# A two-layer hybrid encoder on one core: the weighted sum of the dilated branch's three patterns formed by Pool instead of DVE

## The chip, the cores and the metric

The kernel runs on one core of a Trainium2 chip. Its engines are TensorE (PE, matrix products and transposes), VectorE (DVE), ScalarE (ACT), GpSimd (Pool) and SyncE (SP), which here issues most DMAs. Each runs its own list of instructions in order and waits on semaphores. The metric is the device time of one execution in microseconds (us).

## The reference, cut to what matters

Two layers. In each, one input projection feeds four token mixers (A, B, C, D) and four gates. The outputs, projected and gated, are summed, projected and added to x; a gated MLP with a short convolution follows. The change concerns mixer C, which runs the same banded attention with three dilation patterns and weights their outputs per head with a softmax over the three log-sum-exps:

```
def dilated_attention(c_qkv, pos, q_norm, k_norm):
    ...
    for j, (window, r) in enumerate(C_PATTERNS):       # 3 patterns
        ...
        o, lse = banded_attention(strided(q)[:, :, :, None], strided(k), strided(v), strided(pos), ...)
        outs.append(unstrided(o[:, :, :, 0]))
        lses.append(unstrided(lse[:, :, :, 0]))
    w = jax.nn.softmax(jnp.stack(lses, 0), axis=0)
    o = jnp.sum(w[..., None] * jnp.stack(outs, 0).astype(jnp.float32), axis=0)
    return o.reshape(b, s, C_HEADS * HEAD_DIM).astype(c_qkv.dtype)
```

Sequence length is 512, C has 8 heads of 64 columns, all data is float32. So `o` is 512 x 512: four tiles of 128 tokens with 512 columns each, and three such sets go into the sum.

## The kernel before

**Dense work.** `ORDER` (line 130) lists the projections of a layer in the order in which PE does them. Each weight block is cut into tiles of 256 rows; SP loads them into two buffers `raw`. To keep float32 precision each weight tile is split in two: ACT makes the high half `wh` (line 833), DVE the low half `wl = raw - wh` (line 1262), and the same is done with activations (`hTh`/`hTl`, `gTh`/`gTl`). A product is then three matmuls (line 500). A tile of a block is four "slots" of PE, one for each PSUM bank, six matmuls each.

**The order of everything else.** Small work is woven between the slots. Each stream of an engine yields a due time counted in slots, and `together` takes the stream that is due first. This happens when the program is built, so on the chip each engine has one fixed list. The block before the change is `cq` (D's latent queries), then come `gate2a` (16 slots) and `dq0`. Behind `END["cq"]` these things are due:

- DVE: nine steps of an inverse square root by Newton (lines 1293 to 1299), four pairs of instructions that scale cq (lines 1470 and 1472, the second raises `normed`), the low halves of the turned cq tiles (line 1620), splits of weight tiles (1262), and the combination of C (`c_combine`): weights from the statistics (1395 to 1413), then for each of the four tiles three products with a weight broadcast over 64 columns (1419) and two sums (1422). The last sum of each tile raises `combined`.
- PE: a turn is a set of 128x128 transposes (line 530) into the single PSUM bank `TD`. It waits until ACT and DVE have taken the last one out (`td_act`, `td_dve`). Four turns of cq stand 6, 8, 10 and 12 slots behind `END["cq"]`, four of the combined C tiles at 14, 15.5, 17 and 18.5; the latter wait for `combined`.
- ACT: high halves of turned tiles (1032 for cq, 993 for C), and the eviction of `gate2a` (881) at 13.3 slots, which waits for `combined` of the fourth tile since its target `merged` lies over `oC`:

```
yield from gates_out("gate2a", merged[:, 0:4, :], combined.at(l, 4))
```

- Pool fills two buffers before the layers begin and has nothing to do in them.

Of the kernel before, what the change touches and what calls it, by code (L numbers as in the profile page):

```python
# [16 lines left out]
ALU = mybir.AluOpType  # L17
# [4 lines left out]
P = 128  # L22
# [3 lines left out]
HD = 64  # L26
# [80 lines left out]
class Own:  # L107
# [12 lines left out]
    pj_dve=108, sq_used=60, normed=53, combined=4, sublayer_normed=4, h_normed=8, td_ready=69, td_act=69, td_dve=69, nt_ready=16, nt_act=16,  # L120
    nt_dve=16, ta_ready=136, ta_act=136, ta_dve=136, q_padded=64, s_ready=144, s_biased=144, p_ready=144, b_mixed=16, o_ready=128, o_out=24,
    gains_in=1, ssum=16, lam_dot=1, lam_exp=1, c_diff=1, c_exp=1, merged_sum=24, merged_hi=8, merged_lo=8, conv_mid=44,
    e_ready=22, hidden_val=22, hidden_hi=22, hidden_lo=22, act_step=189, dve_step=497, params_in=16, direct_in=8,
    x_moved=2, c0_moved=6,
)

# [30 lines left out]
def build(nc, io):  # L157
    ctx = ExitStack()
    with ctx:
        _build(nc, io, ctx)  # L160
# [42 lines left out]
def _build(nc, io, ctx):  # L203
    def sb(name, shape, dt=F32):
        return ctx.enter_context(nc.sbuf_tensor("s_" + name, shape, dt))
# [3 lines left out]
    def signal(name, before=0, unit=1):  # L209
        s = Signal(ctx.enter_context(nc.semaphore(name)), before, EACH.get(name, 0), unit)  # L210
        signals[name] = s
        return s
# [25 lines left out]
    stat = sb("stat", [P, 16, 32])  # L238
# [5 lines left out]
    def in_work(at, n, **dims):  # L244

        names = " ".join(dims)
        return work[:, at:at + n].rearrange(f"p ({names} n) -> p {names} n", **dims)
# [7 lines left out]
    oC = in_work(AD + 6144, 6144, j=3, t=4)  # L255
# [42 lines left out]
    combined = signal("combined")  # L298
# [21 lines left out]
    lam_exp = signal("lam_exp")  # L320
    c_diff = signal("c_diff")
    c_exp = signal("c_exp")
    merged_sum = signal("merged_sum")
    merged_hi = signal("merged_hi")
    merged_lo = signal("merged_lo")
    conv_mid = signal("conv_mid")
    e_ready = signal("e_ready")
    hidden_val = signal("hidden_val")
    hidden_hi = signal("hidden_hi")
    hidden_lo = signal("hidden_lo")  # L330
    act_step = signal("act_step", before=1)
    dve_step = signal("dve_step", before=1)
    params_in = signal("params_in", before=16, unit=16)
    direct_in = signal("direct_in", unit=16)
# [15 lines left out]
    def layers(eng):  # L350
        return eng.Fori(0, DEPTH)
# [78 lines left out]
    @block_.sync  # L430
    def _(sp):
        for dst, src in ((work[:, 512:1024].bitcast(I32), io["positions"][0, :].partition_broadcast(P)),
                         (work[:, 256:260].bitcast(I32), io["positions"].rearrange("a (t p) -> p (a t)", p=P)),
                         (work[:, 260:264].bitcast(I32), io["positions"].rearrange("a (p r) -> p (a r)", r=RES)),
                         (consts[:], io["k_consts"])):
            sp.dma_start(dst, src, allow_slow_non_contiguous=True).then_inc(small_in, 16)
        sp.dma_start(x_sb, io["x"].rearrange("a (t p) n -> p (a t) n", p=P)).then_inc(x_in, 16)
        sp.wait_ge(rows_clear, 1)
        for dst, src in list(parameter_rows(0))[6:]:
            sp.dma_start(dst, src, allow_slow_non_contiguous=True).then_inc(params_in.handle, params_in.unit)  # L440
        for dst, src in ((near[:], io["k_near"]), (work[:, 0:256].rearrange("p (m n) -> p m n", m=2), io["k_mask_c12"])):
            sp.dma_start(dst, src).then_inc(setup_in, 16)
        with layers(sp) as l:
            for k, (_when, (pieces, chunks, cols, _last)) in enumerate(weight_tiles(l)):

                sp.wait_ge(*tile_split.at(l, k - 1))
                dst = raw[:, k % 2, 0:chunks * cols].rearrange("p (c n) -> p c n", c=chunks)
                for at, n, src in pieces:
                    sp.dma_start(dst[:, :, at:at + n], src).then_inc(*(raw_landed[k % 2]).up())

        sp.wait_ge(*pj_dve.at(DEPTH, 0))
        sp.dma_start(io["y"].rearrange("a (t p) n -> p (a t) n", p=P), x_sb).then_inc(out_done, 16)
        sp.wait_ge(out_done, 16)


    @block_.gpsimd
    def _(pool):

        for s in (tile_split, tile_used, pj_ready, pj_dve, td_act, td_dve, ta_act, ta_dve, s_biased, o_out, act_step, dve_step):
            pool.sem_inc(s.handle, s.before)  # L460
        pool.memset(rows[:], 1.0).then_inc(rows_clear, 1)
        pool.memset(q_pad[:], 0.0).then_inc(pad_clear, 1)


    @block_.tensor
# [736 lines left out]
    def _(dve):  # L1202
        v = nc.vector
# [47 lines left out]
        with layers(dve) as l:  # L1251
            n_ready, n_turn, n_unit, n_att, n_hi, n_act, n_norm = [0], [0], [0], [0], [0], [0], [0]
            own = Own(pj_dve)
# [57 lines left out]
            def heads(ap, h, w=None):  # L1311
                return ap.rearrange("p (h n) -> p h n", h=h)

            def over(col, n):

                return col.unsqueeze(2).to_broadcast([P, col.shape[1], n])
# [72 lines left out]
            def c_combine():  # L1389

                begin = END["cq"] + 0.3
                yield begin
                dve.wait_ge(*c0_moved.at(l, 6))
                dve.wait_ge(*own.done(l))
                v.tensor_tensor(stat[:, 15, :], stat[:, 5, :], stat[:, 6, :], ALU.min).then_inc(*dve_step.up(own))
                dve.wait_ge(*own.done(l))
                v.tensor_tensor(stat[:, 15, :], stat[:, 15, :], stat[:, 7, :], ALU.min).then_inc(*dve_step.up(own))
                for j in range(3):
                    dve.wait_ge(*own.done(l))
                    v.tensor_tensor(stat[:, 12 + j, :], stat[:, 15, :], stat[:, 5 + j, :], ALU.subtract).then_inc(*(c_diff if j == 2 else dve_step).up(own))  # L1400
                yield begin + 1.2
                dve.wait_ge(*c_exp.at(l, 1))
                dve.wait_ge(*own.done(l))
                v.tensor_tensor(stat[:, 8:11, :], stat[:, 8:11, :], stat[:, 12:15, :], ALU.mult).then_inc(*dve_step.up(own))
                dve.wait_ge(*own.done(l))
                v.tensor_tensor(stat[:, 8, :], stat[:, 8, :], stat[:, 9, :], ALU.add).then_inc(*dve_step.up(own))
                dve.wait_ge(*own.done(l))
                v.tensor_tensor(stat[:, 8, :], stat[:, 8, :], stat[:, 10, :], ALU.add).then_inc(*dve_step.up(own))
                dve.wait_ge(*own.done(l))
                v.reciprocal(stat[:, 8, :], stat[:, 8, :]).then_inc(*dve_step.up(own))  # L1410
                for j in range(3):
                    dve.wait_ge(*own.done(l))
                    v.tensor_tensor(stat[:, 12 + j, :], stat[:, 12 + j, :], stat[:, 8, :], ALU.mult).then_inc(*dve_step.up(own))
                for t in range(4):
                    for j in range(3):
                        yield begin + 5 + 2 * t + 0.6 * j
                        o = oC[:, j, t, :]
                        dve.wait_ge(*own.done(l))
                        v.tensor_tensor(heads(o, 8), heads(o, 8), over(stat[:, 12 + j, 8 * t:8 * t + 8], HD), ALU.mult).then_inc(*dve_step.up(own))  # L1419
                        if j:  # L1420
                            dve.wait_ge(*own.done(l))
                            v.tensor_tensor(oC[:, 0, t, :], oC[:, 0, t, :], o, ALU.add).then_inc(*(combined if j == 2 else dve_step).up(own))

            def add_to_x(names):
                for cb, name in enumerate(names):
# [303 lines left out]
            def attentions():  # L1729
# [44 lines left out]
                for j in (1, 2):  # L1774
                    yield from attention(f"C{j}", biased_residues(j), keep_residues(j), 2)
                yield from c_combine()
                yield from attention("D", biased_d, tile_of_heads(False), 8, tile_at=0)
                yield from attention("A", biased_near(0, A_SLOPES, floor=lambda u: sink[:, u % 8:u % 8 + 1]), tile_of_heads(True), 8,
# [47 lines left out]
```

## Time and profile before

| | |
|---|---|
| time, median of 3 runs | 2898.15 us (2895.33 to 2903.14) |
| profiled execution | span 2911.1 us; the profile gives no other time of it |
| mean granted TensorE clock | 0.960 |
| PE busy | 2729.1 us, 94% |
| DVE busy | 1567.2 us, 54% |
| ACT busy | 1221.1 us, 42% |
| Pool busy | 1.5 us |

A busy share is an average over the whole span. Rows in order of time begin with the start in us from the span's start and the duration in us; "x3" is three merged instructions, and a bracket holds the engine's idle time before the row and who ended it. The granted clock stands in tenths of full speed or as a share (1.00 is 2.4 GHz, 0.50 is 1.2 GHz).

### The profile page before, as it was taken

The page shows a single profiled execution, that of the slowest core. Times are in us where ns is not written, and L with a number is a line of the kernel's source. Part 1 is how long each engine was busy: PE and PEld are TensorE (multiplying, and loading weights), DVE is VectorE, ACT ScalarE, POOL GpSimd, SP SyncE. Part 2 cuts the span into 40 slices and gives each one's busy share as a digit, 9 for nine tenths or more (in the row PEclk, how much of TensorE's full clock was granted, in tenths as well). Part 3 has the DMA queues.
Part 4 walks back from the last instruction along what each step waited for, and adds up shares of the span by engine and source line. Part 5 has one row for each costly group of instructions (what it writes and reads, how often), then busy time and mean ns, then how long its engine had stood idle before and what let it go on. Part 6 is the DMA issues. An engine that isn't in the chain of part 4 may idle for free.

```text
span 2911.1 us, 44313 instructions
## 1 busy us (share of the span) xinstructions
PE 2729.1 (94%) x12974; PEld 2274.5 (78%) x12974; DVE 1567.2 (54%) x3226; ACT 1221.1 (42%) x2487; POOL 1.5 (0%) x6
## 2 busy tenths in 40 slices
PE   5999989889999998999989999898899999899998
PEld 4899877667777787888868998775677777788887
DVE  5454476435546546564655554754355545564745
ACT  4455544335543234342435455433355342342422
POOL 0000000000000000000000000000000000000000
PEclk9999999879999999999999999998699999999999
DMA  4212212001112332333332122220012223223332
GB/s 157 81 51 82 75 56 92 8 8 52 59 60 72 103 100 77 99 94 101 96 103 73 56 77 76 68 80 1 22 45 66 62 72 110 79 95 102 95 95 94
DMA packets 141881, 217.58 MB, mean 75 GB/s; under 512 B 14841, under 2 KB 69451, under 8 KB 141259
## 3 DMA queue, kind: packets, MB, share of 16 engines
q1 hardware_dynamic: 132585, 200.62, 22.2%
q10 hardware_dynamic: 9058, 14.06, 1.5%
q8 instruction: 116, 1.90, 0.3%
q14 instruction: 122, 1.00, 0.1%
HBM read 206.20 MB, written 8.45 MB: 74 GB/s over the span
## 4 chain that ended last, share of the span: by engine, by line
PE 78%; DVE 9%; issue 5%; ACT 5%; ACTq 1%; DMA 1%; DVEq 0%; SPq 0%
PE bank L500 60%; PE bank L693 5%; PE bank L530 5%; PE bank L683 5%; PE bank L737 2%; ACT s_wh L833 1%; DVE s_wl L1262 1%; PE bank L728 1%; DVE s_gTl L1589 1%; ACT s_work L1082 1%; DMA s_raw<-in_w_in 1%; DVE s_work L1419 1%; ACT s_gTh L993 1%; PE bank L566 1%; ACTq L933 1%
## 5 line engine op out<-in xcount | busy, mean ns | idle before, releaser
L1262 DVE TENSOR_TENSOR s_wl<-s_raw,s_wh 128x1024 fp32r<-128x1024 f32 (+2 forms) x376 | 454.4, 1209 | 518.3 <-ACT s_wh L833 515.2
L833 ACT ACTIVATE s_wh<-s_raw 128x1024 fp32r<-128x1024 f32 (+2 forms) x376 | 392.9, 1045 | 587.2 <-PE bank L500 569.2
L500 PE MATMUL bank<-s_hTh,s_wh 128*128 128x512 f32 x1216 | 502.7, 413 | 9.7 <-DVE s_work L1356 9.7
L500 PE MATMUL bank<-s_hTh,s_wl 128*128 128x512 f32 x1216 | 479.3, 394 | 0.0
L500 PE MATMUL bank<-s_hTl,s_wh 128*128 128x512 f32 x1216 | 478.7, 394 | 0.0
L500 PE MATMUL bank<-s_wh,s_hTh 128*128 128x512 f32 (+1 forms) x1088 | 474.4, 436 | 0.0
L500 PE MATMUL bank<-s_wh,s_hTl 128*128 128x512 f32 (+1 forms) x1088 | 427.2, 393 | 0.0
L500 PE MATMUL bank<-s_wl,s_hTh 128*128 128x512 f32 (+1 forms) x1088 | 426.6, 392 | 0.0
L530 PEld LDWEIGHTS bank<-s_consts,s_work 128*128 128x128 f32 (+1 forms) x1432 | 186.3, 149 | 176.2 <-issue 42.2
L530 PE MATMUL bank<-s_consts,s_work 128*128 128x128 f32 (+1 forms) x1432 | 240.1, 293 | 73.6 <-DVE s_gTl L1589 29.4
L1082 ACT ACTIVATE s_work<-s_work,s_stat 128x128 f32<-128x128 f32 (+3 forms) x320 | 167.2, 523 | 302.9 <-DVE s_work L1748 152.3
L500 PEld LDWEIGHTS bank<-s_hTh,s_wh 128*128 128x128 f32 x1216 | 231.9, 191 | 69.3 <-DVE s_work L1356 12.9
L500 PEld LDWEIGHTS bank<-s_wh,s_hTh 128*128 128x128 f32 x1088 | 252.6, 232 | 31.7 <-issue 0.5
L500 PEld LDWEIGHTS bank<-s_hTl,s_wh 128*128 128x128 f32 x1216 | 231.8, 191 | 56.7 <-issue 11.0
L500 PEld LDWEIGHTS bank<-s_wl,s_hTh 128*128 128x128 f32 x1088 | 254.4, 234 | 27.4 <-issue 0.6
L500 PEld LDWEIGHTS bank<-s_wh,s_hTl 128*128 128x128 f32 x1088 | 252.2, 232 | 27.0
L500 PEld LDWEIGHTS bank<-s_hTh,s_wl 128*128 128x128 f32 x1216 | 231.2, 190 | 49.8
L1673 DVE COPY s_work<-bank 128x128 f32<-128x128 f32 (+1 forms) x224 | 77.8, 347 | 237.8 <-ACT s_work L1070 156.4
L500 PE MATMUL bank<-s_wh,s_gTh 128*128 128x512 f32 (+1 forms) x432 | 165.9, 384 | 0.0
L500 PE MATMUL bank<-s_wh,s_gTl 128*128 128x512 f32 (+1 forms) x432 | 165.5, 383 | 0.0
L500 PE MATMUL bank<-s_wl,s_gTh 128*128 128x512 f32 (+1 forms) x432 | 165.4, 383 | 0.0
L1070 ACT ACTIVATE s_work<-bank 128x256 f32<-128x256 f32 (+1 forms) x224 | 77.8, 347 | 96.9 <-PE bank L530 94.8
(181 smaller groups left out, 3432.7 us busy)
## 6 DMA issues: line engine op xcount, KB each, us to landing
s_raw<-in_w_in SPq DMA_DIRECT2D x168, 512.0 KB, 3.4
s_raw<-in_ffn_w_up SPq DMA_DIRECT2D x176, 256.0 KB, 2.9
s_raw<-in_ffn_w_down SPq DMA_DIRECT2D x44, 512.0 KB, 3.6
s_raw<-in_w_branch SPq DMA_DIRECT2D x32, 512.0 KB, 3.7
s_raw<-in_w_o SPq DMA_DIRECT2D x16, 512.0 KB, 3.6
x_keep<-s_work ACTq DMA_DIRECT2D x2, 2048.0 KB, 7.3
s_raw<-in_w_in SPq DMA_DIRECT2D x16, 256.0 KB, 2.9
s_work<-x_keep ACTq DMA_DIRECT2D x2, 2048.0 KB, 8.7
```

The lines of the kernel that those rows point to most:

```text
L500: last = mm(PJ[b][:, 0:width], st, mv, start=i == 0 and n == 1, stop=i == ntiles - 1 and n == 3 * chunks)
L530: last = nc.tensor.transpose(dst[0:m, (at + n) * P:(at + n) * P + k], src, ident[0:k, 0:k])
L566: last = nc.tensor.transpose(dst[:, t * P:t * P + P], h_sb[:, t, P * c:P * c + P], ident)
L683: last = mm(out, st, mv, start=start, stop=stop)
L693: last = mm(out, st, mv, start=True, stop=True)
L728: last = mm(O1[:, P * h:P * h + P], probsT[:, pair % 2, P * k:P * k + P], vB[:, k, P * h:P * h + P], start=k == 0, stop=k == 3)
L737: mm(out, st, mv, start=True, stop=True).then_inc(*s_ready.up())
L833: a(wh[:, k % 3, 0:n], raw[:, s, 0:n], ACT.Copy).then_inc(*hi_split.up(own))
L1070: a(probsT[:, u % 2, P * lo:P * mid], src[:, P * lo:P * mid], ACT.Copy).then_inc(*ta_act.up(own))
L1082: a(probs[:, u % 2, x0:x0 + w], scores[:, u % 2, x0:x0 + w], ACT.Exp, scale=-1.0, bias=stat[:, mins, c:c + 1], accum_out=stat[:, sums, c:c ...
L1262: v.tensor_tensor(wl[:, k % 3, 0:n], raw[:, k % 2, 0:n], wh[:, k % 3, 0:n].bitcast(F32), ALU.subtract).then_inc(*tile_split.up(own))
L1673: v.tensor_copy(probsT[:, u % 2, P * mid:P * hi], src[:, P * mid:P * hi]).then_inc(*ta_dve.up(own))
```

## The change

The 12 products and 8 sums of a layer leave DVE's list and stand in Pool's, in the same order and with the same operands. DVE's last weight product now raises a new semaphore, `c_weighed`, on which Pool waits once a layer; a second one, `c_part`, orders each sum behind the products and the sum that it reads. Pool raises `combined`. The due times of the 20 instructions are gone: Pool has one stream.

```diff
@@ def _(pool) @@
+        with layers(pool) as l:
+            tt, n = nc.gpsimd.tensor_tensor, 0
+            pool.wait_ge(*c_weighed.at(l, 1))
+            for t in range(4):
+                for j in range(3):
+                    o, weight = oC[:, j, t, :].rearrange("p (h n) -> p h n", h=8), stat[:, 12 + j, 8 * t:8 * t + 8]
+                    tt(o, o, weight.unsqueeze(2).to_broadcast([P, 8, HD]), ALU.mult).then_inc(*c_part.up())
+                    n += 1
+                    if j:
+                        pool.wait_ge(*c_part.at(l, n))
+                        n += j == 1
+                        tt(oC[:, 0, t, :], oC[:, 0, t, :], oC[:, j, t, :], ALU.add).then_inc(*(combined if j == 2 else c_part).up())
@@ def c_combine() @@
                 for j in range(3):
                     dve.wait_ge(*own.done(l))
-                    v.tensor_tensor(stat[:, 12 + j, :], stat[:, 12 + j, :], stat[:, 8, :], ALU.mult).then_inc(*dve_step.up(own))
-                for t in range(4):
-                    for j in range(3):
-                        yield begin + 5 + 2 * t + 0.6 * j
-                        o = oC[:, j, t, :]
-                        dve.wait_ge(*own.done(l))
-                        v.tensor_tensor(heads(o, 8), heads(o, 8), over(stat[:, 12 + j, 8 * t:8 * t + 8], HD), ALU.mult).then_inc(*dve_step.up(own))
-                        if j:
-                            dve.wait_ge(*own.done(l))
-                            v.tensor_tensor(oC[:, 0, t, :], oC[:, 0, t, :], o, ALU.add).then_inc(*(combined if j == 2 else dve_step).up(own))
+                    v.tensor_tensor(stat[:, 12 + j, :], stat[:, 12 + j, :], stat[:, 8, :], ALU.mult).then_inc(*(c_weighed if j == 2 else dve_step).up(own))
```

DVE's list before, from the split of the weight tile in gate2a to the low halves of the first turned cq tile (ISA rows are waits):

```order
L1262 TENSOR_TENSOR s_wl<-s_raw,s_wh 128x1024
L1418 ISA
L1419 TENSOR_TENSOR s_work<-s_work,s_stat 128x512
L1418 ISA
L1419 TENSOR_TENSOR s_work<-s_work,s_stat 128x512
L1421 ISA
L1422 TENSOR_TENSOR s_work<-s_work 128x512
L1418 ISA
L1419 TENSOR_TENSOR s_work<-s_work,s_stat 128x512
L1421 ISA
L1422 TENSOR_TENSOR s_work<-s_work 128x512
L1574 ISA
```

The same place after the change (its line numbers are higher by 7 or 16):

```order
L1278 TENSOR_TENSOR s_wl<-s_raw,s_wh 128x1024
L1581 ISA
L1626 ISA
L1627 SCALAR_TENSOR_TENSOR s_gTl<-bank,s_prm,s_gTh 128x128
L1626 ISA
L1627 SCALAR_TENSOR_TENSOR s_gTl<-bank,s_prm,s_gTh 128x128
```

The five instructions of tile 0 are gone from between the split and the low halves, and those of tiles 1 to 3 from behind the low halves of cq's tiles. Everything else on DVE keeps its order. On Pool, after the change, a layer begins so:

```order
L473 TENSOR_TENSOR s_work<-s_work,s_stat 128x512 [waits c_weighed]
L473 TENSOR_TENSOR s_work<-s_work,s_stat 128x512
L476 ISA
L478 TENSOR_TENSOR s_work<-s_work 128x512 [waits c_part]
L473 TENSOR_TENSOR s_work<-s_work,s_stat 128x512
L476 ISA
L478 TENSOR_TENSOR s_work<-s_work 128x512 [waits c_part]
```

That is tile 0: products of patterns 0 and 1, their sum, the product of pattern 2 and the second sum; it is repeated for tiles 1 to 3.

## Rows read from the trace of the kernel before

**Rows 1.** Page, engines: busy us (share of the span) xinstructions.
```profile
PE 2729.1 (94%) x12974; PEld 2274.5 (78%) x12974; DVE 1567.2 (54%) x3226; ACT 1221.1 (42%) x2487; POOL 1.5 (0%) x6
```

**Rows 2.** Windows at the combination in the first layer; the header names the columns.
```profile
core 0: us, PE busy (x) PEld busy (x) DVE busy (x) ACT busy (x) POOL busy (x), PEclk, DMA share, GB/s
...
396.00:400.00 4.00, 1.56 (x7) 0.94 (x5) 3.86 (x6) 0.08 (x1) 0.00 (x0) 0.97 0.17 49
400.00:404.00 4.00, 1.94 (x6) 1.69 (x7) 3.76 (x8) 0.86 (x3) 0.00 (x0) 0.50 0.00 0
404.00:408.00 4.00, 4.00 (x15) 3.17 (x14) 3.79 (x8) 1.08 (x3) 0.00 (x0) 0.68 0.00 0
408.00:412.00 4.00, 2.53 (x12) 1.72 (x10) 3.79 (x7) 1.00 (x3) 0.00 (x0) 1.00 0.34 98
```

**Rows 3.** Chain of waits, 391 to 417 us: start us, us, what.
```profile
397.24 0.70 DVE s_work L1419
...
398.70 0.70 DVE s_work L1422
...
400.88 0.36 DVE s_gTl L1620
```

**Rows 4.** DVE in order of time in the second layer: start us, us, engine, instruction.
```profile
1834.99 0.65 DVE L1413 TENSOR_TENSOR s_stat<-s_stat 128x32 f32<-128x32 f32 x3
```

**Rows 5.** DVE in order of time, first layer; in brackets idle time before, and releaser.
```profile
390.93 0.65 DVE L1413 TENSOR_TENSOR s_stat<-s_stat 128x32 f32<-128x32 f32 x3
391.61 0.16 DVE L1293 TENSOR_TENSOR s_stat<-s_stat 128x4 f32<-128x4 f32 x1
...
393.38 0.19 DVE L1470 TENSOR_TENSOR s_krr<-s_work,s_rope_rows 128x32 f32<-128x32 f32 x1
393.61 0.42 DVE L1472 TENSOR_SCALAR s_work<-s_work,s_stat 128x384 f32<-128x384 f32 x1
...
395.99 1.22 DVE L1262 TENSOR_TENSOR s_wl<-s_raw,s_wh 128x1024 fp32r<-128x1024 f32 x1
...
400.88 1.12 DVE L1620 SCALAR_TENSOR_TENSOR s_gTl<-bank,s_prm,s_gTh 128x128 fp32r<-128x128 f32 x3
...
415.38 0.69 DVE L1422 TENSOR_TENSOR s_work<-s_work 128x512 f32<-128x512 f32 x1
```

**Rows 6.** PE in order of time, first layer: the turns of the latents and combined tiles.
```profile
394.25 0.54 PE L530 MATMUL bank<-s_consts,s_work 128*128 128x128 f32 x3 [0.72 <-DVE s_work L1472]
...
402.06 0.90 PE L530 MATMUL bank<-s_consts,s_work 128*128 128x128 f32 x3 [4.50 <-DVE s_gTl L1620]
...
407.28 0.49 PE L530 MATMUL bank<-s_consts,s_work 128*128 128x128 f32 x3
...
412.50 0.55 PE L530 MATMUL bank<-s_consts,s_work 128*128 128x128 f32 x3 [1.97 <-DVE s_gTl L1620]
...
417.29 0.66 PE L530 MATMUL bank<-s_consts,s_work 128*128 128x128 f32 x4
...
420.41 0.66 PE L530 MATMUL bank<-s_consts,s_work 128*128 128x128 f32 x4 [1.08 <-DVE s_gTl L1589]
```

**Rows 7.** ACT in order of time, first layer: gate evictions and the first high halves.
```profile
416.27 1.23 ACT L881 ACTIVATE s_work<-bank 128x512 f32<-128x512 f32 x2 [1.52 <-DVE s_work L1422]
418.06 1.08 ACT L993 ACTIVATE s_gTh<-bank 128x512 fp32r<-128x512 f32 x1 [0.57 <-PE bank L530]
```

**Rows 8.** The two lines of the combination: duration ns min/median/max, first and last start.
```profile
L1419 DVE TENSOR_TENSOR s_work<-s_work,s_stat x24: 691/692/693, 397.2 to 1858.7; 128x512 f32<-128x512 f32 x24
...
L1422 DVE TENSOR_TENSOR s_work<-s_work x16: 691/692/694, 398.7 to 1859.4; 128x512 f32<-128x512 f32 x16
```

**Rows 9.** Pool's fills: line, engine, operation, count, busy us, mean ns.
```profile
L462 POOL MEMSET s_q_pad<- 128x1024 f32 x1 | 1.0, 957 | 0.0
L461 POOL MEMSET s_rows<- 128x384 f32 x1 | 0.4, 418 | 1.2 <-issue 1.2
```

**Rows 10.** DVE in order of time: a one-input scaling of 256 columns.
```profile
363.43 0.35 DVE L1464 TENSOR_SCALAR s_work<-s_work,s_stat 128x256 f32<-128x256 f32 x1
```

More of the change, by code:

```diff
@@ L122 @@
     gains_in=1, ssum=16, lam_dot=1, lam_exp=1, c_diff=1, c_exp=1, merged_sum=24, merged_hi=8, merged_lo=8, conv_mid=44,
-    e_ready=22, hidden_val=22, hidden_hi=22, hidden_lo=22, act_step=189, dve_step=497, params_in=16, direct_in=8,
+    e_ready=22, hidden_val=22, hidden_hi=22, hidden_lo=22, act_step=189, dve_step=480, c_weighed=1, c_part=16, params_in=16, direct_in=8,
     x_moved=2, c0_moved=6,
@@ L322, in _build @@
     c_exp = signal("c_exp")
+    c_weighed = signal("c_weighed")
+    c_part = signal("c_part")
     merged_sum = signal("merged_sum")
```

## The prediction

> **What bounds the kernel now.** I read the engine line of the page first, then the windows around the combination of C, then the chain of waits there, then each engine's instructions in order of time. TensorE is busy for 94% of the span and DVE for 54% [rows 1], so DVE work is free on average. The average hides this stage. In the windows from 396 to 412 us DVE is busy for 3.8 of every 4 us, while TensorE falls to 1.56, 1.94 and 2.53 of 4 us in three of the four, and its granted clock to 0.50 in the second [rows 2]. The chain of waits of this stretch is a list of DVE instructions, one behind the other [rows 3]. So here, twice in a run (the second layer repeats the rows 1444 us later [rows 4]), DVE sets the pace.
>
> In order of time [rows 5]: the last of the three small products that make the weights ends at 391.6. Behind it stand nine Newton steps for cq (0.16 us each, up to 393.4), four pairs that scale cq (0.19 and 0.42 us), and the split of a weight tile (1.22 us, up to 397.2). Only then come the combination of tile 0 (five instructions of 0.70 us) and the low halves of cq's first turned tile at 400.9. PE, which had made the turn of tile 0 at 394.25 and two slots of matmuls, stands 4.50 us until 402.06 for those low halves, and 1.97 us until 412.50 for the third ones [rows 6]. The fourth combined tile is ready at 415.38 + 0.69 = 416.07; ACT waits for it (its gate evictions start at 416.27 [rows 7]). So two things end here: the latents' turns, and the fourth combined tile.
>
> **What the change takes away.** 12 products and 8 sums a layer: 20 instructions, 24 and 16 in the run [rows 8], each 0.69 us and 0.72 from start to start: 14.4 us of DVE a layer. They stand in the chain [rows 3]. Were nothing put in their place, the low halves of tile 0 would start at 397.3 in place of 400.9 and PE would turn tile 1 at about 398.5; with 3.2 us for each later turn (the turn and its two slots of matmuls took 412.50 - 1.97 - 407.28 = 3.25 us at full clock) it would come to its first turn of combined tiles at about 408.5 instead of 417.29 [rows 6]: 8.8 us a layer. That is the most that the removal can give, 18 us in all.
>
> **What it adds.** Pool does the same 20 instructions, in one run from the moment the weights are there (391.6): one semaphore starts it, nothing paces it. The trace has no arithmetic of Pool. Its nearest rows are two fills, 0.42 us for 384 columns and 0.96 for 1024 [rows 9]: 0.84 ns a column and 0.10 us fixed, so one pass over 512 columns is 0.53 us. A product reads two operands and writes one. If the three streams run side by side it is 0.53 us, the lower end; one after the other 1.39, the upper end; two passes 0.96. I take 1.2: between two passes and three, since each sum also waits until the instructions before it have ended.
> For this the Trainium skill (GPSIMD Engine Reference, 3.1 Elementwise) has a measured 4497 ns for 2048 columns against 2293 on the vector engine; a quarter is 1.12 us, an estimate from that page. No run here shows it yet, and with it in place of 1.2 the sum below would be 3 us smaller.
>
> **Does it run beside DVE?** DVE's own rows show how it reads SBUF. A two-input product takes 0.19 us for 32 columns and 0.69 for 512, 1.04 ns a column with two values read. The one-input scaling takes 0.35 us for 256 columns and 0.42 for 384 [rows 5, 10], about 0.55 ns a column: it too reads two values in the time of one step. So both kinds use two read streams, and Pool would need a third and fourth. Nothing in this trace has both engines at work, so the bounds are: no hindrance at all (0), or every such DVE instruction waits for the Pool instruction that is under way, and Pool's next waits for it. I take the second, as the rows show DVE never faster than two streams, and price it from them.
> The Trainium skill says it outright (SBUF — State Buffer, Who interferes with whom): a vector instruction with two SBUF inputs, or one in a two-port mode, contends with a GpSimd instruction that reads SBUF, and the later one is blocked until the first has finished. No row here tests it; by that rule the time would be that of the forecast, without it that of the first rival.
>
> **The sum, per layer.** Behind the weights DVE has 18 instructions of this kind before the low halves: nine Newton steps, four pairs, one split. Each waits for one Pool instruction: 9 x (1.2 + 0.16) = 12.2; 4 x (1.2 + 0.19) + 4 x (1.2 + 0.42) = 12.0; 1.2 + 1.22 = 2.4; together 26.7 us with the roundings. The split ends at 391.6 + 26.7 = 418.3 instead of 397.2. The low halves (1.12 us, one input in PSUM, the other in SBUF, so I let them run free) end at 419.4, when PE can turn tile 1: 17.3 us later than now. From there PE has three turns to its first combined tile. PE has stood before it, as before 402.06: the first interval I take as there, 5.2 us, with the clock at half [rows 2, 6]; the other two 3.2 us each, since no combination lies between. That is 419.4 + 5.2 + 6.4 = 431.0 against 417.29: +13.7 us. Pool has done 18 of its 20 by 418.3 and ends near 421, ten microseconds before PE asks; it hides there. From the first combined tile on, the four turns follow each other by the round PE, ACT, DVE in 3.1 us as now [rows 6, 7], and all later work moves with PE. The one credit is the removed 14.4 us on DVE, and it is within the wait. The move of the sum past the next weight splits is harmless, they stand with DVE and shift with it.
> Two layers: +27.4 us. On the profiled execution that is 2911.1 + 27.4 = 2938.5 (the span is all that it shows; the median of the three runs stands 13 us below, 0.4%). On the median: 2898.15 + 27.4 = 2926. With Pool at 0.96 it is 18 x 0.24 = 4.3 us a layer less, 2917; at 1.39, 3.4 more, 2933. If Pool lets DVE in only where it waits itself (twice a tile), DVE starts its last ten instructions at about 417, and it is 2 to 3 us a layer more: 2931.
>
> **Rivals.**
> 1. *The engines don't hinder each other, and the gain is given back at the fourth tile: no change.* DVE is then as fast as worked out above and PE comes to the combined tiles at 408.5. But ACT's gate evictions wait for the fourth combined tile, and the high halves of the combined tiles stand behind them on ACT, so PE can't make the second turn. Pool gives that tile at 391.6 + 20 x 1.2 = 415.6, against 416.07 now. From there ACT's start (0.2), two evictions (1.23), the high halves (1.08) and what lies between their end at 419.14 and the turn at 420.41 (1.27, the low halves) make 3.8 us: 419.4 against 420.41 [rows 6, 7], -1.0. PE has then stood for some 9 us and its clock is low again; a turn and 12 matmuls took 5.2 us at 402.06 after such a wait, some 5.0 with dq0's narrower ones, where the round takes 3.1: +1.9. Together +0.9 a layer, +2 in all: 2900. For it speaks that the rows prove no hindrance.
> 2. *Faster: Pool is quick and unhindered.* The fourth tile decides: with the +0.9 at 1.2 us an instruction, nothing is lost or won at 1.16, and each tenth below is 2 us a layer. From 0.94 down it is over 0.3% faster; at 0.85 the tile is there at 408.6, -6.1 a layer, 2886; at 0.7, DVE's own rate, it no longer holds anything and the 8.8 us come through, 2881. Against it: that asks for at most two passes at the rate of Pool's own fills, with nothing for the waits before the sums, and for no hindrance as well.
> 3. *Unhindered, but Pool is slow,* 1.6 to 2.0 us an instruction, above the upper end (a broadcast operand, a hand-over before each sum). The fourth tile comes at 423.6 to 431.6: +8 to +16 a layer, 2914 to 2930. It ends where the forecast does, with another cause.
> 4. That the change doesn't move the work is excluded by the order: Pool has 20 more instructions a layer and DVE 20 fewer.
>
> **How the numbers follow.** Forecast 0.56, first rival 0.20, second 0.12, third 0.12. About 0.3% (8.7 us) is what a measurement of this kernel can tell from no change: faster is below 2889.5, slower above 2906.8. The second rival gives faster, 0.12; the first gives the same, and with it the quick edge of the third, 0.21; slower is left with 0.67. The forecast's own range is 2914 to 2942; for 8 in 10 the range has to take in the first rival: 2893 to 2942.
>
> **What would show it.** Step by step, in the first layer: Pool's products start near 391.7, with about 1.2 us from start to start where DVE is idle, 1.4 where it is not. The Newton steps, spaced by 0.20 us now, lie 1.3 to 1.4 apart. The split that ends at 397.2 ends near 418. PE's wait for cq's scaling (0.72 us now) grows to some 13 us and the one for the low halves (4.50) to 7 or more. DVE shows as longer busy or as idle with no releaser, whichever way the profile puts a held instruction. The forecast is wrong if the Newton steps keep their 0.20 us; then the start of ACT's gate evictions against 416.27 tells the first rival from the second and third. It is wrong in size if a small instruction is let in before a Pool instruction ends.

## The result, and the profile after

Slower by 0.63%: median of 5 runs 2923.24 us (2911.16 to 2927.62) against 2902.59 (2895.33 to 2909.71), ratio 1.0063 with the interval [1.0039, 1.0088]. In a second comparison it is 2923.65 (6 runs) against 2904.33, ratio 1.0071 [1.0051, 1.0091].

The two profiled executions can't be set side by side as a whole: that of after has a span of 2909.0 us (it is the fastest of its five), that of before 2911.1, which is longer than any of the five times of before. So the reading goes by landmarks within a layer, and first by those around the change. The page's engine line of after:

```profile
PE 2713.9 (93%) x12974; PEld 2261.7 (78%) x12974; DVE 1566.1 (54%) x3186; ACT 1221.1 (42%) x2487; POOL 48.4 (2%) x46
```

DVE has 40 instructions fewer, 27.7 us by [rows 8], and is busy as long as in [rows 1]: something gave the time back. Pool in order of time, first layer, with columns as in [rows 5]; the first five rows and the last:

```profile
392.48 2.05 POOL L473 TENSOR_TENSOR s_work<-s_work,s_stat 128x512 f32<-128x512 f32 x2 [389.48 <-DVE s_stat L1429]
394.60 1.26 POOL L478 TENSOR_TENSOR s_work<-s_work 128x512 f32<-128x512 f32 x1
395.83 1.04 POOL L473 TENSOR_TENSOR s_work<-s_work,s_stat 128x512 f32<-128x512 f32 x1
396.95 1.26 POOL L478 TENSOR_TENSOR s_work<-s_work 128x512 f32<-128x512 f32 x1
398.17 2.04 POOL L473 TENSOR_TENSOR s_work<-s_work,s_stat 128x512 f32<-128x512 f32 x2
...
415.26 1.28 POOL L478 TENSOR_TENSOR s_work<-s_work 128x512 f32<-128x512 f32 x1
```

Twenty instructions from 392.48 to 416.54, 1.20 us each: 1.04 for most products, 1.26 for a sum. DVE in the same stretch:

```profile
391.75 0.65 DVE L1429 TENSOR_TENSOR s_stat<-s_stat 128x32 f32<-128x32 f32 x3
392.43 0.16 DVE L1309 TENSOR_TENSOR s_stat<-s_stat 128x4 f32<-128x4 f32 x1
392.63 0.91 DVE L1312 SCALAR_TENSOR_TENSOR s_stat<-s_stat 128x4 f32<-128x4 f32 x1
393.57 0.97 DVE L1315 SCALAR_TENSOR_TENSOR s_stat<-s_stat 128x4 f32<-128x4 f32 x1
394.58 0.16 DVE L1309 TENSOR_TENSOR s_stat<-s_stat 128x4 f32<-128x4 f32 x1
394.77 1.11 DVE L1312 SCALAR_TENSOR_TENSOR s_stat<-s_stat 128x4 f32<-128x4 f32 x1
...
399.26 0.99 DVE L1477 TENSOR_TENSOR s_krr<-s_work,s_rope_rows 128x32 f32<-128x32 f32 x1
400.30 1.47 DVE L1479 TENSOR_SCALAR s_work<-s_work,s_stat 128x384 f32<-128x384 f32 x1
...
408.64 2.28 DVE L1278 TENSOR_TENSOR s_wl<-s_raw,s_wh 128x1024 fp32r<-128x1024 f32 x1
410.96 1.12 DVE L1627 SCALAR_TENSOR_TENSOR s_gTl<-bank,s_prm,s_gTh 128x128 fp32r<-128x128 f32 x3
```

The Newton steps that took 0.16 us [rows 5] take 0.91 to 1.11, the pairs 0.9 to 1.2 and 1.1 to 1.5, the split 2.28. The profile puts the time for which an instruction is held into its own duration, which is why DVE's busy sum did not fall. The low halves (L1627), with one input in PSUM, keep their 1.12. The 18 instructions behind the weights last from 392.43 to 410.92: 18.5 us where they took 5.6. PE's turns, to be read beside [rows 6]:

```profile
402.00 0.90 PE L546 MATMUL bank<-s_consts,s_work 128*128 128x128 f32 x3 [7.61 <-DVE s_work L1479]
...
412.13 0.90 PE L546 MATMUL bank<-s_consts,s_work 128*128 128x128 f32 x3 [4.16 <-DVE s_gTl L1627]
...
417.95 0.54 PE L546 MATMUL bank<-s_consts,s_work 128*128 128x128 f32 x3
...
424.23 0.66 PE L546 MATMUL bank<-s_consts,s_work 128*128 128x128 f32 x4
...
427.38 0.66 PE L546 MATMUL bank<-s_consts,s_work 128*128 128x128 f32 x4 [1.10 <-DVE s_gTl L1596]
```

PE stands 7.61 us ahead of the latents' first turn, where it stood 0.72 in before, and 4.16 ahead of the second (4.50 in before). In two of the four windows below the granted clock is near 0.50, in before in one of them (columns as in [rows 2]):

```profile
core 0: us, PE busy (x) PEld busy (x) DVE busy (x) ACT busy (x) POOL busy (x), PEclk, DMA share, GB/s
...
396.00:400.00 4.00, 0.00 (x0) 0.00 (x0) 3.86 (x5) 0.00 (x0) 3.92 (x4) 0.70 0.00 0
400.00:404.00 4.00, 2.00 (x7) 1.72 (x8) 3.90 (x4) 0.92 (x3) 3.84 (x5) 0.50 0.00 0
404.00:408.00 4.00, 3.98 (x10) 2.62 (x8) 3.86 (x5) 0.18 (x1) 3.92 (x5) 0.52 0.00 0
408.00:412.00 4.00, 0.00 (x0) 0.00 (x0) 3.89 (x5) 0.00 (x0) 3.92 (x4) 0.90 0.00 0
```

**Landmarks.** ACT's exponential of C's log-sum-exps (387.56 in before, 388.39 in after) stands just ahead of the weights, and the first 512-column exponential of D ends the stage. ACT's rows of before:

```profile
387.56 0.28 ACT L1172 ACTIVATE s_stat<-s_stat 128x96 f32<-128x96 f32 x1 [0.16 <-DVE s_stat L1400]
...
528.43 0.72 ACT L1082 ACTIVATE s_work<-s_work,s_stat 128x512 f32<-128x512 f32 x1 [1.91 <-DVE s_work L1748]
```

and of after:

```profile
388.39 0.28 ACT L1188 ACTIVATE s_stat<-s_stat 128x96 f32<-128x96 f32 x1 [0.17 <-DVE s_stat L1416]
...
534.20 0.72 ACT L1098 ACTIVATE s_work<-s_work,s_stat 128x512 f32<-128x512 f32 x1 [1.91 <-DVE s_work L1755]
```

A combined turn is PE's turn of one of the four combined tiles. From the exponential to the start of the fourth it is 39.1 us in before, in both layers; the first combined turn moved by (424.23 - 388.39) - (417.29 - 387.56) = 6.1. The table has the fourth turn of every run, its shift summed over both layers, what the runs measured, and the stage from the exponential to D's (all in us). Its kernels are explained in the next section.

| kernel | fourth turn, layer 1, 2 | shift, both | ratio to before, and in us of 2900 | stage 1, 2 |
|---|---|---|---|---|
| before | 39.10, 39.10 | | | 140.9, 138.9 |
| after | 45.26, 44.85 | +11.9 | 1.0063 [1.0039, 1.0088], +18 | 145.8, 147.0 |
| after, again | 44.84, 45.14 | +11.8 | 1.0071 [1.0051, 1.0091], +21 | 144.9, 145.9 |
| e_reads | 56.03, 56.06 | +33.9 | 1.0110 [1.0067, 1.0154], +32 | 155.9, 158.3 |
| e_steady | 58.83, 58.80 | +39.4 | one run: +45 | 159.5, 159.6 |
| e_fills | 42.64, 42.64 | +7.1 | 1.0027 [1.0007, 1.0048], +8 | 142.6, 142.6 |
| e_late | 45.29, 45.58 | +12.7 | 1.0053 [1.0028, 1.0078], +15 | 145.2, 147.8 |
| e_before_gates | 39.11, 39.13 | 0.0 | 1.0002 [0.9983, 1.0022], +1 | 138.9, 139.1 |
| e_after_gates | 44.75, 43.77 | +10.3 | 1.0047 [1.0025, 1.0069], +14 | 144.8, 144.9 |
| e_late_gates | 35.65, 35.85 | -6.7 | 0.9990 [0.9967, 1.0012], -3 | 137.4, 137.9 |
| e_shared | 35.98, 35.89 | -6.3 | 0.9947 [0.9926, 0.9967], -15 | 136.3, 136.8 |
| e_shared, again | 35.97, 35.92 | -6.3 | 0.9966 [0.9948, 0.9985], -10 | 137.2, 135.7 |
| e_shared_now | 41.76, 41.07 | +4.6 | 1.0014 [0.9991, 1.0037], +4 | 141.8, 141.1 |

The fourth turn repeats within some tenths of a us (once 1.0), the stage within 3 us. Behind it comes D's attention, up to A's first exponential (that of the sink, 128x1): it takes 120 to 135 us, in before 135.2 and 133.3 us, in after 127.9 and 124.0, and in the same kernel again 134.3 and 129.0. The 7 and 9 us that after has less there than before are what hides the change in the two spans. The stage is longer where the mean granted clock over it is lower: in the first layer 0.71 in before (528 to 664 us) and 0.79 in after (534 to 662), but 0.72 in after again (532 to 667) and 0.71 in e_late_gates, which takes 135.2 us too.

### The profile page after: what moved, and what is told of

Read it like the earlier page. It is cut to its first block, busy times and chain, and to the rows that moved or that the text cites. A ratio compares the mean times of both kernels' runs of the same rounds, so it can differ in the third digit from the quotient of the medians.

```text
span 2909.0 us, 44300 instructions
## 1 busy us (share of the span) xinstructions
PE 2713.9 (93%) x12974; PEld 2261.7 (78%) x12974; DVE 1566.1 (54%) x3186; ACT 1221.1 (42%) x2487; POOL 48.4 (2%) x46
## 4 chain that ended last, share of the span: by engine, by line
PE 78%; DVE 8%; issue 5%; ACT 5%; ACTq 1%; DMA 1%; DVEq 1%; SPq 0%
PE bank L516 61%; PE bank L546 5%; PE bank L709 5%; PE bank L699 4%; PE bank L753 2%; ACT s_wh L849 1%; DVE s_wl L1278 1%; PE bank L744 1%; DVE s_gTl L1596 1%; ACT s_work L1098 1%; ACT s_gTh L1009 1%; PE bank L582 1%; ACTq L949 1%; DVE s_stat L1312 0%; DVE s_stat L1315 0%
## 5 line engine op out<-in xcount | busy, mean ns | idle before, releaser
L516 PEld LDWEIGHTS bank<-s_wl,s_hTh 128*128 128x128 f32 x1088 | 254.7, 234 | 27.4 <-issue 0.6
```

The source lines that it names most:

```text
L516: last = mm(PJ[b][:, 0:width], st, mv, start=i == 0 and n == 1, stop=i == ntiles - 1 and n == 3 * chunks)
```

## The experiments

The theory: while Pool reads its operands from SBUF, a DVE instruction with two SBUF inputs, or a one-input scaling, is held until Pool's instruction has ended, and the chain to PE's turns gets longer. The rivals: Pool's combined tiles come too late (1 and 3 of the prediction), or it is something else in the new order.

**Pool beside an unchanged DVE.** Three kernels leave before's combination on DVE and give Pool work on idle buffers that nobody uses; DVE only waits for its end ahead of D's attention. The code is shortened, indices too, to what Pool does. e_reads has the 12 products and 8 sums with the waits of after. e_steady has 20 products of two full tiles, each waiting only for the one six back. e_fills has nine groups of a small product and three fills.

```diff
+            pool.wait_ge(*c_weighed.at(l, 1))
 e_reads:
+                    nc.gpsimd.tensor_tensor(scratch[k + j], bias_b[:, j], weight_broadcast, ALU.mult)
+                        nc.gpsimd.tensor_tensor(scratch[k], scratch[k], scratch[k + j], ALU.add)
 e_steady, 20 times:
+                nc.gpsimd.tensor_tensor(scratch[t % 6], bias_b[t % 4], bias_b[(t + 1) % 4], ALU.mult)
 e_fills, 9 times:
+                nc.gpsimd.tensor_tensor(scratch[0, 0:8], bias_b[0, 0:8], bias_b[1, 0:8], ALU.mult)
+                pool.memset(scratch[1], 1.0); pool.memset(scratch[2:4], 1.0); pool.memset(scratch[4:6], 1.0)
```

> The kernel before, with DVE's combination left where it was; Pool runs in addition 12 products and 8 sums of 128x512 on idle buffers, started by the same last weight product. Nobody uses what it computes. Turn-taking at SBUF: the 18 DVE instructions from the first Newton step to the end of the weight split take 18 to 19 us as in the changed kernel, in place of 5.6; the combination is held too until Pool is done near 416, so the fourth tile comes about 17 us later than before: some +30 us in all (2930). No hindrance (the change was slow only because Pool's result comes late): the 18 instructions keep their 5.6 us and the time is that of before.

e_reads: 2932.08 us, ratio 1.0110 [1.0067, 1.0154]. With DVE's list as before and no result of Pool awaited, the 18 instructions take the same 18.5 us as in after. DVE in order of time:

```profile
390.90 0.16 DVE L1310 TENSOR_TENSOR s_stat<-s_stat 128x4 f32<-128x4 f32 x1
391.10 0.92 DVE L1313 SCALAR_TENSOR_TENSOR s_stat<-s_stat 128x4 f32<-128x4 f32 x1
392.05 0.97 DVE L1316 SCALAR_TENSOR_TENSOR s_stat<-s_stat 128x4 f32<-128x4 f32 x1
...
407.11 2.29 DVE L1279 TENSOR_TENSOR s_wl<-s_raw,s_wh 128x1024 fp32r<-128x1024 f32 x1
409.43 2.86 DVE L1436 TENSOR_TENSOR s_work<-s_work,s_stat 128x512 f32<-128x512 f32 x2
412.33 1.63 DVE L1439 TENSOR_TENSOR s_work<-s_work 128x512 f32<-128x512 f32 x1
```

The same instructions are held by the same amounts. This shows the hindrance apart from the change, without its order and without its late result. DVE's own 0.69 us products take 1.43 and its sum 1.63 beside Pool, so here the combination is held as well.

> As the first, but Pool's 20 instructions are products of two full tiles, none of which has to wait for the one ahead (waits reach six instructions back). In the changed kernel three of the nine Newton steps, the squares, took 0.16 us and the other six about 1.0. If a square slips in because it comes just when Pool waits ahead of a sum: here no square does, and the 18 instructions take 18 x 1.2, about 22 us. If a square is free because both its inputs are the same tensor: three of nine keep 0.16 us here too.

e_steady: 2949.83 us in one run, its profiled one. DVE:

```profile
393.04 0.16 DVE L1303 TENSOR_TENSOR s_stat<-s_stat 128x4 f32<-128x4 f32 x1
393.24 1.16 DVE L1306 SCALAR_TENSOR_TENSOR s_stat<-s_stat 128x4 f32<-128x4 f32 x1
394.43 1.20 DVE L1309 SCALAR_TENSOR_TENSOR s_stat<-s_stat 128x4 f32<-128x4 f32 x1
395.67 1.19 DVE L1303 TENSOR_TENSOR s_stat<-s_stat 128x4 f32<-128x4 f32 x1
...
411.97 1.35 DVE L1482 TENSOR_SCALAR s_work<-s_work,s_stat 128x384 f32<-128x384 f32 x1
413.25 2.28 DVE L1272 TENSOR_TENSOR s_wl<-s_raw,s_wh 128x1024 fp32r<-128x1024 f32 x1
```

Only the first square (L1303, the Newton step that multiplies the estimate by itself) is free: Pool starts at 393.09, after it. The other two, free in after and e_reads, take 1.19 here, where Pool has no wait. So it was not their form that let them in; in after they start at 394.58 and 396.92, just as Pool has ended its products and waits ahead of a sum (394.60 and 396.95). The 18 take 22.5 us, as expected.

> As the last one, but Pool's 20 instructions are replaced by 27 fills (memset, 512 or 1024 columns, about 22 us of Pool in a layer) with a product of 8 columns ahead of each three. Fills write SBUF and read nothing. If DVE is held by Pool's reads: the 18 instructions stay within 1 us or so of their 5.6 us (the small products can hold one now and then) and the time is that of before. If any work of Pool in SBUF holds DVE: 15 us or more for the 18, and some +25 us in all.

e_fills: 2910.38 us (10 runs), ratio 1.0027 [1.0007, 1.0048]. DVE:

```profile
391.84 0.16 DVE L1309 SCALAR_TENSOR_TENSOR s_stat<-s_stat 128x4 f32<-128x4 f32 x1
...
393.42 0.19 DVE L1483 TENSOR_TENSOR s_krr<-s_work,s_rope_rows 128x32 f32<-128x32 f32 x1
393.64 0.71 DVE L1485 TENSOR_SCALAR s_work<-s_work,s_stat 128x384 f32<-128x384 f32 x1
394.39 0.19 DVE L1483 TENSOR_TENSOR s_krr<-s_work,s_rope_rows 128x32 f32<-128x32 f32 x1
394.62 2.27 DVE L1485 TENSOR_SCALAR s_work<-s_work,s_stat 128x384 f32<-128x384 f32 x1
...
399.55 1.23 DVE L1275 TENSOR_TENSOR s_wl<-s_raw,s_wh 128x1024 fp32r<-128x1024 f32 x1
```

Beside fills, which only write, every two-input instruction keeps its time, the Newton steps and the 1024-column split too. Only the one-input scaling is held: 0.71 to 2.27 us in place of 0.42. So the 18 take 9.1 us and the run is 0.27% slower: the expectation, within 1 us of 5.6 and the time of before, did not allow for the scalings. That Pool is busy is not enough to hold the two-input ones; it must read. The Trainium skill (SBUF — State Buffer, Who interferes with whom) says that an instruction with two SBUF inputs contends with a Pool instruction that reads SBUF and not with one that only writes it, and that a tensor_scalar can run in a mode that takes both pairs of ports and contends with Pool; these rows agree.

**The start of Pool, and who waits for the tile.** In e_late Pool also waits for the weight split that ends the 18 instructions (L48 below). In the three "gates" kernels ACT's eviction of gate2a waits for combined tile by tile, its last two due 0.7 and 1.7 slots later (G); e_before_gates and e_after_gates have G alone, e_late_gates both.

```diff
 L48, Pool:
             pool.wait_ge(*c_weighed.at(l, 1))
+            pool.wait_ge(*tile_split.at(l, 48))
 G, ACT:
-                    yield END[name] - 2.7 + m
-                    if m == 0:
+                    yield END[name] - 2.7 + (0, 1, 2.7, 4.7)[m] if by_tile else END[name] - 2.7 + m
+                    if by_tile:
+                        act.wait_ge(*combined.at(l, m + 1))
+                    elif m == 0:
                         act.wait_ge(*after)
```

> The changed kernel, but Pool waits in addition for the weight split that ends the 18 DVE instructions (gate2a's fourth tile), so it starts about 5.7 us later and they are not held. Turn-taking: the 18 take 5.6 us again, PE makes the second latent turn near 399 instead of 412, but Pool's fourth tile comes near 421 and now holds ACT's gate evictions and with them the second combined turn, near 427 (the changed kernel: 427.4). So the time is that of the changed kernel within 0.2%, with PE's wait moved from the latents' turns to the combined tiles. If the loss were in Pool's late result alone, it would be about 6 us a layer slower than the changed kernel.

e_late: 2921.81 us, ratio 1.0053 [1.0028, 1.0078]: as slow as after within the intervals, and for another reason. DVE's 18 instructions are back at 5.6 us (391.77 to 397.37). Pool runs from 397.44 to 421.30. PE's turns of combined tiles:

```profile
408.01 0.66 PE L547 MATMUL bank<-s_consts,s_work 128*128 128x128 f32 x4
...
425.06 1.11 PE L547 MATMUL bank<-s_consts,s_work 128*128 128x128 f32 x4 [15.01 <-DVE s_gTl L1597]
```

and ACT's gate evictions:

```profile
421.49 1.23 ACT L898 ACTIVATE s_work<-bank 128x512 f32<-128x512 f32 x2 [14.38 <-POOL s_work L479]
422.75 1.07 ACT L1010 ACTIVATE s_gTh<-bank 128x512 fp32r<-128x512 f32 x1
```

The first combined turn comes at 408.0, 20.3 us behind the exponential where before needs 29.7: the prediction's "what the removal can give" (8.8) is there in full, 9.5. Then PE stands 15.01 us, since the high halves stand on ACT behind evictions that wait for the fourth tile. That is the chain of rivals 1 and 3; the 3.8 us that they put between Pool's fourth tile and the second turn are 425.06 - 421.30 = 3.8.

> The kernel before, with one edit on ACT: each of gate2a's four evictions waits for its own combined tile instead of all for the fourth, and the last two are due 0.7 and 1.7 slots later, behind the high halves of the combined tiles. A control for the next two. In the kernel before DVE's own list ends at 419 with the combination, the low halves and the rotation, and PE comes to the first combined tile only at 417.3: the fourth tile is not what is late. So no change, within 0.3%. If ACT's wait for the fourth tile (3.0 us in two waits) were on the path: 1 to 2 us a layer faster.

> The same edit on the changed kernel. By the trace after, Pool's fourth tile is ready at 416.5 and ACT's first gate eviction starts at 423.4: the wait is over before ACT comes to it. Turn-taking: the time of the changed kernel, +0.6% against before, within 0.2%. If Pool's late result were the cause: back to the time of before or faster.

e_before_gates: 2905.74, ratio 1.0002 [0.9983, 1.0022]; e_after_gates: 2919.16, 1.0047 [1.0025, 1.0069]. The edit alone is worth nothing in before, and in after the fourth turn moves by 0.5 and 1.1 us, where after's own two profiles differ by 0.4 and 0.3: the late tile is not what costs after its 12. In after the evictions start at 423.37, seven us behind Pool's last sum at 416.54, with no wait on it.

> Pool starts behind the 18 DVE instructions, as in the late variant, and ACT's evictions wait tile by tile. If the late variant's 15.0 us of PE at the second combined turn came from ACT's wait for the fourth tile, and DVE's 18 instructions are free again, both losses are gone: combined tiles at about 403.8, 409.9, 415.6 and 421.3, PE's four combined turns at 408, 412 to 415.5, 416 to 419 and 421.5 to 422, against 426.7 for the last one before. 5 us a layer faster than before, 2893 (-0.35%). If one of the two explanations is wrong it stays at the changed kernel's +0.5%.

e_late_gates: 2903.99, ratio 0.9990 [0.9967, 1.0012], which missed the 0.35% expected. The turns of combined tiles are at 408.07, 415.56, 420.31 and 423.43. The second waits 5.45 us for its low halves on DVE: the rope instructions ahead of them, 0.23 us where they run free, now lay beside Pool, and five took 0.96 to 1.31, so that the low halves started at 414.43. The fourth was expected at 421.5 to 422. The stage is 3.4 us a layer shorter than before's by the fourth turn. By the turns the run should gain 6.7 us; it shows 3, with an interval from 10 faster to 3 slower.

**The work shared.** Pool keeps the 12 products and starts late; DVE makes the 8 sums, due where Pool is nearly done with the products they need; G as above. e_shared_now is the same with Pool started at once. The edit on DVE (Pool's sums are taken out):

```diff
+                for t in range(4):
+                    for j in (1, 2):
+                        yield END["cq"] + 9.8 + 2.2 * t + 0.1 * j
+                        dve.wait_ge(*c_part.at(l, 3 * t + j + 1))
+                        dve.wait_ge(*own.done(l))
+                        v.tensor_tensor(oC[:, 0, t, :], oC[:, 0, t, :], oC[:, j, t, :], ALU.add).then_inc(*(combined if j == 2 else dve_step).up(own))
```

> As the last, but DVE forms the eight sums (0.69 us each against Pool's 1.26) and Pool the twelve products only (1.04 to 1.12). Turn-taking: the pair's total is 12 x 1.1 + 8 x 0.7 = 19 us instead of 24, so the fourth tile is ready near 417 and PE's last combined turn at about 418, 8 us a layer earlier than before: 2886 (-0.55%). If each hand-over between the two engines costs more than 0.5 us, or DVE's sums wait for a product with other work behind them, it is no faster than the last variant.

e_shared: 2888.27 us (12 runs), ratio 0.9947 [0.9926, 0.9967]. A second time:

> The shared variant a second time. In its profile the combination's stage (from C's exponentials to D's first exponential) was 2.3 us a layer shorter than in the kernel before with ACT's edit (136.3 and 136.8 us against 138.9 and 139.1), but D's attention in the first layer took 119.7 us where eight other kernels took 128 to 135. If D's stage is a matter of each execution: a time 0.2 to 0.5% below before, and another length of D's stage in the profile. If the shared order shortens it: again 0.5% below, and again about 120.

2893.22 us, ratio 0.9966 [0.9948, 0.9985]. Both times it is faster than before, and so than after. PE's turns of combined tiles:

```profile
411.80 0.66 PE L541 MATMUL bank<-s_consts,s_work 128*128 128x128 f32 x4 [0.61 <-DVE s_gTl L1632]
...
416.93 0.97 PE L541 MATMUL bank<-s_consts,s_work 128*128 128x128 f32 x4 [3.09 <-DVE s_gTl L1601]
...
424.17 0.66 PE L541 MATMUL bank<-s_consts,s_work 128*128 128x128 f32 x4 [1.43 <-DVE s_gTl L1601]
```

The largest wait ahead of these turns is 3.09 us, and the fourth turn is 3.1 and 3.2 us earlier than in before. It was expected 8 us earlier, at 418, with the fourth tile ready near 417: it comes at 424.17, the tile's last sum ends at 421.80. So the time came out as forecast (2886) and the shift did not: of the 15 and 10 us gained in the two comparisons the turns show 6. The second comparison was to tell whether the order also shortens D's attention (again 0.5% and about 120 us) or chance did (0.2 to 0.5%, another length). With 0.34% and 122.3 us it tells neither. Pool's 12 products take 14.58 us; two pairs of sums lie beside them and take 1.4 us a sum, the other two pairs come later and take 0.71.

> The shared variant with Pool's twelve products started as soon as the weights are there, as in the changed kernel. Turn-taking: they run for some 13 us beside the 18 DVE instructions, each of which up to the twelfth is held for about 1.0 us; the split ends near 409 instead of 397, the second latent turn comes near 410 and the combination's stage is 5 us a layer longer than in the shared variant: +0.1 to 0.2% against before. If the late start is worth nothing: as the shared variant.

> The changed kernel a second time, beside the shared variants on one chip. From C's exponentials to D's first exponential its profile has 145.8 and 147.0 us against 138.9 and 139.1 with the work on DVE: 15 us in the two layers, so I expect +0.5 to 0.6% against before, and 145 to 147 us again for that stage, whatever D's stage does.

e_shared_now: 2909.21, ratio 1.0014 [0.9991, 1.0037], not told apart from before; against e_shared beside it (2893.22) it is 16 us slower. Its fourth turn lies 5.8 and 5.2 us behind that of e_shared, for the start alone. DVE is held until Pool's products end at 402.9, its Newton squares too (0.97; Pool has no sums to wait for), and the split ends at 405.6 and not near 409 as expected: the last instructions ran free. again_after is the changed kernel beside it, told above.

## Why the prediction was right or wrong

**Right in kind and in the time, 2926 forecast and 2923 measured; wrong in the size of one term, and the time so near by luck in part.**

- *DVE sets the pace here, and the removal can give 8.8 us.* Right: with Pool kept away, 9.5 (e_late).
- *Pool takes 1.2 us an instruction.* Right as a mean, 1.20; a product 1.04, a sum 1.26. The Trainium skill's figure is for an add (GPSIMD Engine Reference, 3.1 Elementwise); the estimate from it, a quarter, is 1.12, which is 0.14 below the sum measured here.
- *Each of 18 instructions waits for one of Pool's; 26.7 us.* The mechanism is right (e_reads), the size is the failed step: 18.5. The hold was put at 21.1 us, 1.17 for each of 18. Measured are 18.5 - 5.6 = 12.9, 0.86 for each of 15. Three squares ran free, one ahead of Pool's start and two where Pool waited ahead of a sum, 3.5 us less; and the duration of DVE's instruction hardly adds to Pool's: the 15 held ones follow each other 1.19 us apart on average, where Pool's own starts lie 1.15 apart ((409.80 - 392.48) / 15) and the forecast had 1.51. That is 4.7 us less. The forecast had named the first way, let in only where Pool waits, but as a loss.
- *PE waits 13 and at least 7 us.* It waits 7.61 and 4.16. The second turn was to come 27.8 us behind the weights and came after 412.13 - 392.40 = 19.7.
- *The intervals 5.2, 3.2, 3.2.* 5.82, 3.14, 3.14: right to 0.5. So +13.7 became 13.7 - 8.2 + 0.5 = 6.0 (measured 6.1 in the first layer), and two layers are 12 and not 27.
- *Pool's end hides.* Right: 416.54, PE's first combined turn at 424.23.
- *Rivals.* No hindrance (1, 2, 3) is excluded by the Newton rows and e_reads. The tile's path of rivals 1 and 3 exists and decides once Pool starts late (e_late); G takes it away, but then DVE's later work is held (e_late_gates). The sum of rival 3 left out the 0.9 us of the low clock that rival 1 has: at 1.6 to 2.0 us an instruction it would be +9 to +17 a layer, 2916 to 2932.

**What stays open.** The comparison says +18 and +21 us, the turns say +12. The first interval (+11 to +26) holds 12, the second (+15 to +26) does not. By the stage it is +13 (4.9 and 8.1) and +11, and 2 more against the stage of e_before_gates. No profile shows where the 6 to 9 us between turn and run lie. D's attention is no longer in after's profiles than in the others: over both layers it takes 251.9 and 263.3 us in the two profiles of after, 268.5 in before and 261.1 in e_before_gates, and two executions of one kernel differ there by 11, more than the amount sought. e_shared has such a gap too, -6 by the turns and -15 and -10 by the runs: both of its profiles show a short D stage in the first layer (119.7 and 122.3 us, the first of them at a mean granted clock of 0.83), and ordinary ones in the second (131.9 and 133.7). Whether the stage ahead sets this, or chance, no run here tells. That the forecast time came so near is luck in two parts. It added 27.4 us where 18 to 21 were measured: a term some 8 us a layer too large stood in for a part that the forecast did not have. And it added them to 2898.15, the median of three runs of before, where five runs have 2902.59.

## What to carry to other kernels

Work moved from DVE to Pool need not be taken off DVE if both read SBUF: here each neighbour on DVE with two SBUF inputs, and each one-input scaling, paid up to about one Pool instruction, however small it was itself. So look at what urgent small instructions DVE has while Pool would run, start Pool behind them, give it only the part that nobody awaits soon, and let the consumer wait tile by tile (e_shared did all three together; of the start alone e_shared_now shows the worth). And where another stage varies by more than the effect, measure from landmark to landmark beside the change, and let many runs say what reaches the end.

## What the runs showed of the hardware

- A held DVE instruction is shown as busy: 0.16 us became 0.91 to 1.11 in after and 1.19 in e_steady, and in after the sum over the engine fell by 1.1 us with 27.7 us of work gone.
- Holding works both ways: in e_reads, where DVE makes 512-column products beside it, Pool's sums take 1.59 us in place of 1.26.
- Pool's product with an operand broadcast over 64 columns is quicker (1.04 us) than its sum of two full tiles (1.26); the 20 products of two full tiles in e_steady take 26.90 us, 1.35 each, with DVE's large instructions beside them.
- A one-input scaling is held by Pool's fills, up to 2.27 us, longer than one 1024-column fill (0.96); two-input instructions are not (0.16, 0.19 and 1.23 us there, as in before).
